# Four pieces of the first gate vector in a two-layer decoder trunk: scaled by ScalarE and summed by GpSimd instead of VectorE

## The reference, cut to what matters

```python
c_act = jax.nn.silu(c)
for l in range(DEPTH):
    mod = (c_act @ w_ada[l] + b_ada[l])[:, None, :]
    sh1, sc1, gt1, sh2, sc2, gt2 = jnp.split(mod, 6, axis=-1)
    h = x * (1.0 + sc1) + sh1
    y = hybrid_mixer(h, positions, w_in[l], attn_sinks[l], g_a[l], g_b[l], w_o[l])
    x = layer_norm(ALPHA * x + (1.0 + gt1) * y, ln1_g[l], ln1_b[l])
    h = x * (1.0 + sc2) + sh2
    y = swiglu(h, w_gate[l], w_up[l], w_down[l])
    x = layer_norm(ALPHA * x + (1.0 + gt2) * y, ln2_g[l], ln2_b[l])
```

## Time and profile before

| | us |
|---|---|
| median of 3 runs | 1275.48 (1275.37 to 1276.41) |
| the profiled execution, its own time | 1276.25 |
| its span from the first to the last instruction | 1274.6 |
| busy PE / DVE / ACT / POOL | 1235.8 / 801.5 / 510.5 / 274.2 |

### The profile page before, as it was taken

One profiled execution on the slowest core, in us unless ns is written; L12 is line 12 of the kernel. 1 busy time (PEld: TensorE's weight loads), 2 busy tenths in 40 slices (PEclk: granted clock), 3 DMA queues, 4 the chain that ended last, 5 costly groups with the idle time before them and its releaser, 6 DMA issues. The chain is left out here.

```text
span 1274.6 us, 18347 instructions
## 1 busy us (share of the span) xinstructions
PE 1235.8 (97%) x6394; PEld 1031.6 (81%) x6394; DVE 801.5 (63%) x1400; ACT 510.5 (40%) x1027; POOL 274.2 (22%) x281
## 2 busy tenths in 40 slices
PE   6999989999999999999999999999999999999997
PEld 5778876889888888888888688778988888888886
DVE  6889997677777764333676699856733355433338
ACT  3555568345232212222145466862643321222220
POOL 4027236600111010000007367570000000000000
PEclk9999999999999999999999999999999999999999
DMA  9672012334878554222523120112232223332211
GB/s 358 240 270 79 33 51 67 132 116 150 279 264 270 193 168 175 90 93 98 171 94 117 66 67 2 37 63 84 75 124 99 97 101 132 99 98 89 94 65 66
DMA packets 44850, 158.30 MB, mean 124 GB/s; under 512 B 5872, under 2 KB 5872, under 8 KB 44784
## 3 DMA queue, kind: packets, MB, share of 16 engines
q1 hardware_dynamic: 30528, 109.07, 24.8%
q0 software_dynamic: 12960, 47.19, 10.9%
q10 hardware_dynamic: 1296, 1.17, 0.3%
HBM read 155.31 MB, written 2.10 MB: 123 GB/s over the span
## 5 line engine op out<-in xcount | busy, mean ns | idle before, releaser
L631 PE MATMUL bank<-hT_hi,w_hi 128*128 128x512 f32 x640 | 249.5, 390 | 0.0
L633 PE MATMUL bank<-hT_hi,w_lo 128*128 128x512 f32 x640 | 249.0, 389 | 0.0
L632 PE MATMUL bank<-hT_lo,w_hi 128*128 128x512 f32 x640 | 249.0, 389 | 0.0
L1967 DVE TENSOR_TENSOR w_lo<-w_raw,w_hi 128x1024 fp32r<-128x1024 f32 x88 | 107.9, 1226 | 147.0 <-ACT w_hi L1434 147.0
L1280 ACT ACTIVATE w_hi<-w_raw 128x1024 fp32r<-128x1024 f32 x96 | 100.7, 1062 | 202.8 <-PE bank L633 189.0
L1434 ACT ACTIVATE w_hi<-w_raw 128x1024 fp32r<-128x1024 f32 x88 | 93.0, 1057 | 161.1 <-PE bank L633 155.8
L631 PE MATMUL bank<-w_hi,hT_hi 128*128 128x512 f32 (+2 forms) x392 | 148.1, 378 | 2.9 <-ACT pq L1316 2.0
L1544 DVE TENSOR_TENSOR w_lo<-w_raw,w_hi 128x1024 fp32r<-128x1024 f32 x88 | 114.1, 1310 | 53.6 <-ACT w_hi L1280 52.2
L633 PE MATMUL bank<-w_hi,hT_lo 128*128 128x512 f32 (+2 forms) x392 | 142.6, 364 | 0.0
L632 PE MATMUL bank<-w_lo,hT_hi 128*128 128x512 f32 (+2 forms) x392 | 142.3, 363 | 0.0
L633 PEld LDWEIGHTS bank<-hT_hi,w_lo 128*128 128x128 f32 x640 | 120.1, 188 | 25.3
(11 more groups left out here) (207 smaller groups left out, 2199.5 us busy)
## 6 DMA issues: line engine op xcount, KB each, us to landing
w_raw<-in_weights SPq DMA_DIRECT2D x184, 512.0 KB, 3.5
ada_w<-in_w_ada POOLq DMA_DIRECT2D x80, 512.0 KB, 5.2
ada_w<-in_w_ada SPq DMA_DIRECT2D x4, 512.0 KB, 6.6
qT<-in_w_ada SPq DMA_DIRECT2D x4, 512.0 KB, 10.0
xs<-in_x SPq DMA_DIRECT2D x4, 512.0 KB, 15.4
g_row<-in_ln_row POOLq DMA_DIRECT2D x4, 512.0 KB, 5.2
b_row<-in_ln_row POOLq DMA_DIRECT2D x4, 512.0 KB, 6.1
trunk_out<-xs SPq DMA_DIRECT2D x8, 256.0 KB, 2.1
```

What stands on the lines that cost most here:

```text
L631: pe.matmul(dst, a_hi, b_hi, start=first, stop=False)
L632: pe.matmul(dst, a_hi, b_lo, start=False, stop=False)
L633: return pe.matmul(dst, a_lo, b_hi, start=False, stop=last)
L1967: nc.vector.tensor_tensor(w_lo[:, s, :], w_raw[:, s, :], w_hi[:, s, :].bitcast(F32), ALU.subtract).then_inc(lo_ready, 1)
```

## The change

Pieces 28 to 31 are no longer multiplied and added by one VectorE instruction each (L1590, a scalar-tensor-tensor of 128x1024). ScalarE multiplies the piece in its slot of `ada_w`, at the end of step 12, 18, 24 or 30 (`scale_aside`), and raises a new semaphore. GpSimd waits for it, adds the piece to the accumulator (`add_aside`), and then issues the fetch as before, which now waits for its own addition. VectorE's four instructions are gone.

```diff
+        aside_scaled = sem("aside_scaled")
...
+            def add_aside(j):
+
+                n = ASIDE_FROM + j
+                acc = ada_acc[:, acc_of(n // KD), :]
+                pool.wait_ge(aside_scaled, j + 1)
+                pool.wait_ge(ada_used, n)
+                nc.gpsimd.tensor_tensor(acc, acc, ada_w[:, n % RING, :], ALU.add).then_inc(ada_used, 1)
...
                     if i in ASIDE_AT and l == 0:
+                        add_aside(ASIDE_AT.index(i))
                         ada_fetch(ASIDE_FROM + RING + ASIDE_AT.index(i) + 1)
                     if i in ROPE_AT:
                         rope(l, 4, ROPE_AT.index(i))
...
+            def scale_aside(j):
+
+                n = ASIDE_FROM + j
+                piece = ada_w[:, n % RING, :]
+                act.wait_ge(ada_in[n % RING], 16 * ((n - 2 * KD) // RING + 1))
+                nc.scalar.activation(piece, piece, ACT.Copy, scale=cc[:, 1, n % KD:n % KD + 1])\
+                    .then_inc(aside_scaled, 1)
...
                     if i in WO_AT:
                         convert(l, WO_P + WO_AT.index(i) + 1)
+                    if i in ASIDE_AT and l == 0:
+                        scale_aside(ASIDE_AT.index(i))
...
-                    if i in ASIDE_AT and l == 0:
-                        n = ASIDE_FROM + ASIDE_AT.index(i)
-                        ada_group(n // KD, n % KD, n % KD + 1)
```

## The result

| | before | after |
|---|---|---|
| median, 10 runs each on the same chips (us) | 1275.57 (1275.29 to 1277.13) | 1279.07 (1278.06 to 1280.08) |
| the profiled execution, its own time | 1276.25 | 1278.30 |
| its span | 1274.6 | 1276.5 |

The changed kernel takes 1.0025 times as long, with a 95% interval of 1.0017 to 1.0034. That is 3.5 us more, where 2.5 was forecast; it lies inside the range (1278.0 was the forecast, 1276.2 to 1279.5 the range), and the interval has the line of 0.2% inside it.

The account below looks back on a forecast made before the run. PE, busy for 97% of the span, was taken as the bound. Delays of 2.5 us at step 15, 0.6 at `split_y`, 0.2 at step 30 and 2.5 at step 31 gave 1275.48 + 2.5 = 1278.0 us, range 1276.2 to 1279.5.

Parts of the forecast that it names:

- The forecast case: Layer 0's heads' loop: GpSimd's additions ahead of the roots delay `scale_y`; +2.5 us, band +1.6 to +3.4, chance 0.72.
- The step 12 chain: Steps 12 to 15: scaling, addition, fetch, rope and root make `scale_y` start at 155.05 instead of 152.59, 2.5 us late.
- A wait of about 4 us for GpSimd: Expected sign in the changed kernel's profile: `scale_y` at step 15 waits this long for GpSimd, near 155.0.
- The step from there to `split_y`: ScalarE from `scale_y` at step 15 to its half of `split_y`: 4.75 us, ending at 159.8, 0.6 us late.
- PE's step 24: PE at 166.89, where it waits for ScalarE: the 0.6 us delay reaches it through VectorE's masks and ScalarE.
- The step 30 chain: Steps 30 to 31: scaling, addition, fetch, root take 5.0 us from 181.6; `scale_y` at 186.6, 2.5 us late.
- Head 63: Mask of the last head in layer 0's loop: near 231.7, the 2.5 us delay kept to the end.
- I find neither operation inside the additions: VectorE's L1754 and L1765 were checked against the times of GpSimd's four additions; holds add nothing to the sum.
- 4.25 us is the most that the change can bring: Layer 0's loop takes 100.25 us, layer 1's without pieces 96.00; the difference was taken as the pieces' full cost.
- A: Rival: ScalarE and GpSimd hide all the work, layer 0 runs like layer 1; -4.2 us, 1271.2, chance 0.05.
- B: Rival: step 15's stall is absorbed, only the last chain costs; -0.3 to about +1.1 us, 1275.2 to 1276.6, chance 0.12.
- C: Rival: additions hold VectorE's L1754 or L1765, or VectorE holds an addition; around +4 us, 1279.5, chance 0.11.

Follow-up runs that it names:

- the second profile: The changed kernel, nothing altered, run once more beside the variants on one chip: median 1279.11 us, ratio 1.0026 to the kernel before; its profiled execution has +3.18 at head 63.
- behind the roots: Changed kernel with GpSimd's additions and fetches placed after the root within the step, the first at step 14: 1276.06 us, ratio 1.0002 to the kernel before.
- The best order: Changed kernel with piece one ahead of the heads, scalings at steps 7, 19, 26, additions after roots, tile 1's rope after root and `sink_difference`: 1271.12 us, ratio 0.9962.
- step 12 alone: Kernel before with only piece 28 moved to ScalarE and GpSimd, the other three left on VectorE; run twice: 1277.72 and 1277.11 us.
- the changed kernel without the hold: Changed kernel with GpSimd's rope of tile 1 waiting for VectorE's small addition of step 15 (`sink_difference`); run twice: 1278.40 and 1279.73 us.

## Why the prediction was right, and where it wasn't

The forecast case came, with its mechanism and place: +2.76 us in the loop, inside the band of +1.6 to +3.4; the median's +3.5 is just beyond the band and inside the range. Times below are the measured ones plus the 0.75 us of the earlier start.

- **The step 12 chain** was right to 0.03 us. Addition, fetch, root and `scale_y` were worked out as 147.34, 150.00, 154.45 and 155.05; they came at 147.36, 150.03, 154.46 and 155.06. "A wait of about 4 us for GpSimd" was 2.45 + 1.62 us in two rows: the first part went to L1774, which was held up inside the same time.
- **The step from there to `split_y`** is the term that was mis-sized. Predicted 159.8 (+0.6), measured 160.10 (+0.9): ScalarE needed 5.04 us and not 4.75, with 0.23 of it in the exponential's wait for a mask. (The 3.7 us of gapless work in the prediction's sum had no row behind them; less the wait and the scaling's 1.05, they measured 3.76.) PE's step 24 then came 0.88 late instead of 0.6, and head 30 stood at +0.47 instead of +0.2.
- **The step 30 chain** was right: 5.0 us worked out, 5.06 measured (181.12 to 186.18); a wait of "some 3 us" was 3.07, PE's idle time "about 3" was 3.46. It adds 2.29 us from head 30 to head 63, where the prediction had 2.3.
- **Head 63** was +2.76 instead of +2.5, and the profiled execution's own time rose by 2.05 us: 2.76, less the 0.75 of the earlier start, to 0.04.
- **The other 0.7 us of the median** had no term. The profiled execution took 1278.30, the median run 1279.07. The runs' clocks and the second profile point at the clock: it can fall behind the idle time that the change makes. The price per fall differs (0.4 us at head 63 in the second profile, 1.3 in the one of step 12). Falls in the loop are shown in five profiles; that they make up the whole 0.7 us in the median is argued from the mean clocks, and not shown run by run. The start of the loop differs between executions too, and a median of 10 doesn't remove that fully.
- **"I find neither operation inside the additions" was true, and too narrow.** L1774 was held by the rope: before by its last operation (0.90 us), now, with VectorE early and the rope pushed back by the addition, by its first two (3.02 us). The prediction asked where the new operations would meet VectorE, and not where the ones that they push would. Here it cost about 0.3 us by the estimate above, because ScalarE had to wait for the root at the same time; with that wait away (behind the roots) meetings of this kind are the likely reason why head 63 stood at +0.06 where -2.5 was worked out. The Trainium skill, SBUF — State Buffer, section "Who interferes with whom", has a VectorE instruction with two SBUF inputs and a GpSimd instruction that reads SBUF shut each other out. The traces agree, with 1.27, 1.45, 2.25 and 2.26 us for an operation that takes 0.17; the rows of 2.60 and 3.02 us go beyond it.
- **"4.25 us is the most that the change can bring"** is wrong as a bound. The best order brought 4.93 in the loop. The yardstick, layer 1's loop, has 1.1 us of holds of its own, so the most that can be won is an estimated 4.25 + 1.1 = 5.35 us (the 0.73 us of hold that the kernel before has at step 15, is inside that). The best order also moves a piece out of the loop; what that is worth by itself wasn't separated.
- **Rivals.** A (all hidden) failed for the reason given: at step 31 `scale_y` waits 3.07 us. B (only the last chain) failed since step 12 costs 1.13 us by itself. C's size, around +4, is near the median's +3.5; its mechanism was there at step 15, with the rope and not an addition, and was worth about 0.3 us of the loop's +2.76.

## What to carry to other kernels

Before work goes to an idle engine, look at what stands behind it in that engine's queue and who waits for it: 2.4 us of addition in front of a 0.56-us root cost about 2.2 us of the kernel's time (2.29 - 0.13), with GpSimd 22% busy. The cure was order, not less work, and it took two orders at once: behind the roots, and away from VectorE's small two-input operations; when one stall is cured, VectorE runs early and meets something new. A new TensorE stall of some microseconds can cost more than its length, since the clock may fall behind it, so time such a change over several runs and look at the clock in more than one profile.

## What the runs showed of the hardware that was not expected

- **A hold can last over two GpSimd operations.** The 128x8 addition took 3.02 us in the changed kernel (149.42 to 152.44), and 3.03 to 3.04 in three more profiles. In these rows and in the one of 2.60 us it begins while GpSimd issues a fetch (149.28 to 149.87; 145.38 to 145.95), and ends with the second operation behind that fetch. The fetch by itself doesn't hold it: where the rope was made to wait, it began at the same point of the fetch and took 0.17 us. In the loops of layer 0 twelve other rows of these small additions (0.86 to 2.26 us) began beside a GpSimd operation already under way, and each ended with that one. Why some holds take in a second operation, no run tells.
- **The clock falls in some executions and not in others of the same kernel.** With step 12 alone the granted clock is 0.50 from 156 to 159 us in one profile and 1.00 in the other; in the changed kernel it has a mean of 0.60 from 188 to 192 us in the second profile and 1.00 in the first. In the loops of layer 0 PE stands idle for 2.2 to 3.6 us (once or in two waits close together) eleven times in seven profiles, and the clock falls behind six of these. The seven profiles without such a wait have no fall in this loop.
- **An early start of an engine isn't kept.** In the changed kernel without the hold, VectorE is 2.8 us earlier at head 16, and at head 30 it is 0.4 us later than with it (+0.87 against +0.47). PE was waiting for the root at that time anyway. Both runs of it had a fall of the clock at step 18, so the exact value at head 30 is not the order's alone.
